# The scan stage with backward tokens in 32-row blocks, and block turns of 128 partitions

## The reference, cut to what matters

```python
m = jnp.einsum('bnihk,bnjhk->bnhij', k_beta, k) * jnp.exp(jnp.where(strict, diff, -jnp.inf))
t_inv = lax.linalg.triangular_solve(m, eye, left_side=True, lower=True, unit_diagonal=True)
u = jnp.einsum('bnhij,bnjhv->bnihv', t_inv, v * beta[..., None])
w = jnp.einsum('bnhij,bnjhk->bnihk', t_inv, k_beta * jnp.exp(g)[..., None])
```

## Time and profile before

| what | value |
| --- | --- |
| runs, median (lowest to highest) | 4532.65 us (4531.85 to 4542.73) |
| profiled execution, span | 4535.4 us |
| PE busy over the span | 3940.0 us (87%) |
| DVE busy | 2176.8 us (48%) |
| ACT busy | 970.4 us (21%) |
| POOL busy | 1048.6 us (23%) |
| scan stages | 571 to 1140 us and 2802 to 3370 us |

### The profile page before, as it was taken

The page is one execution under the profiler, slowest core; times in us unless marked ns, Lnnn a source line. Parts: engine busy times, 40 slices in busy tenths (PEclk is TensorE's granted clock), DMA queues, the critical chain, the costliest instruction groups (busy, mean ns, idle before and its releaser), DMA issues. The chain is left out here.

```text
span 4535.4 us, 81543 instructions
## 1 busy us (share of the span) xinstructions
PE 3940.0 (87%) x34010; PEld 3088.9 (68%) x34010; DVE 2176.8 (48%) x4932; ACT 970.4 (21%) x1898; POOL 1048.6 (23%) x1092
## 2 busy tenths in 40 slices
PE   4999967888777999999779997788869599999994
PEld 3444546676347999999744444566654399999994
DVE  3335046566555445444453341566646544454444
ACT  2233134444110000000033322443431100000001
POOL 0036034453210000011040440445512001000003
PEclk9999978888888999999989998888879799999997
DMA  7556353331528999999664653243233299999995
GB/s 266 173 192 229 127 125 77 77 71 36 192 72 243 276 276 270 280 278 269 183 233 150 241 192 89 71 95 78 66 110 129 105 278 270 274 278 276 271 279 179
DMA packets 822587, 836.27 MB, mean 184 GB/s; under 512 B 92008, under 2 KB 667560, under 8 KB 816076
## 3 DMA queue, kind: packets, MB, share of 16 engines
q1 hardware_dynamic: 740172, 711.10, 52.5%
q10 hardware_dynamic: 70432, 81.03, 5.3%
q0 software_dynamic: 11616, 38.94, 3.8%
HBM read 698.83 MB, written 132.10 MB: 183 GB/s over the span
## 5 line engine op out<-in xcount | busy, mean ns | idle before, releaser
L2525 PE MATMUL ffn_hb<-ffn_xT,ffn_w 128*128 128x144 f32 x8192 | 1055.4, 288 | 11.2 <-DVE ffn_xT L2638 6.5
L2525 PEld LDWEIGHTS ffn_hb<-ffn_xT,ffn_w 128*128 128x128 f32 x8192 | 1025.8, 191 | 14.1 <-DVE ffn_xT L2638 6.7
L521 PE MATMUL front_acc<-front_w,front_xmT 128*128 128x512 f32 (+2 forms) x2304 | 879.2, 541 | 17.7 <-DVE front_xmT L782 17.5
L521 PEld LDWEIGHTS front_acc<-front_w,front_xmT 128*128 128x128 f32 x2304 | 438.2, 192 | 444.7 <-issue 417.7
L2533 PE MATMUL ffn_acc<-ffn_hT,ffn_w 128*128 128x144 f32 x4096 | 550.2, 288 | 0.0
L2533 PEld LDWEIGHTS ffn_acc<-ffn_hT,ffn_w 128*128 128x128 f32 x4096 | 521.4, 191 | 0.8
L2573 ACT ACTIVATE ffn_en<-ffn_hb 128x144 f32<-128x144 f32 x256 | 74.6, 291 | 1483.0 <-PE ffn_hb L2525 1483.0
L2457 POOL DMA_INDIRECT ffn_xe<-scratch_xhat,ffn_g_idx x34 | 34.5, 1015 | 1376.2 <-DVEq L2627 1376.2
L2672 DVE TENSOR_TENSOR ffn_hT<-ffn_en,ffn_hb 128x144 f32<-128x144 f32 x256 | 77.7, 304 | 528.8 <-ACT ffn_en L2573 527.9
L2247 PE MATMUL mixer_acc<-mixer_wout,mixer_oT 128*128 128x512 f32 x576 | 256.6, 604 | 3.2 <-DMA mixer_wout<-in_w_out 1.7
L2596 DVE TENSOR_SCALAR_CACHE_REDUCE ffn_junk<-ffn_row,ffn_pair 128x128 f32<-128x128 f32 (+2 forms) x324 | 245.4, 757 | 6.3 <-DVE ffn_yp L2645 4.9
(11 more groups left out here) (324 smaller groups left out, 5206.0 us busy)
## 6 DMA issues: line engine op xcount, KB each, us to landing
ffn_w<-in_w_e SPq DMA_DIRECT2D x768, 512.0 KB, 6.4
x_res<-in_w_mod SPq DMA_DIRECT2D x40, 1024.0 KB, 5.6
x_res<-scratch_proj SPq DMA_DIRECT2D x36, 768.0 KB, 6.2
scratch_proj<-front_out ACTq DMA_DIRECT2D x90, 256.0 KB, 2.2
ffn_row<-scratch_affT SPq DMA_DIRECT2D x36, 576.0 KB, 6.3
front_w<-in_w_in ACTq DMA_DIRECT2D x8, 2048.0 KB, 12.3
scan_qk<-scratch_qkv SPq DMA_DIRECT2D x16, 1024.0 KB, 9.8
scratch_qkv<-x_res SPq DMA_DIRECT2D x18, 768.0 KB, 3.5
```

The costliest lines, as they stand in the source:

```text
L521: mm = pe.matmul(acc[:, U % 2, 0:size], xmT[:, k, t * P:(t + 1) * P], w[:, n % 2, k, 0:size], start=k == 0, stop=k == KD - 1)
L2525: mm = pe.matmul(hb[:, b, i * CAP:(i + 1) * CAP], w[:, r, k, :], xT[:, s, k, :], start=k == 0, stop=k == KD - 1)
```

## The change

Backward tokens are no longer in reverse over the whole chunk: within each block of 32 rows the order is the scan's, and the two blocks of a chunk stay in storage order. The backward source becomes two blocks of 32 reversed rows, one DMA for each chunk, so a load of n chunks is one forward and n backward DMAs (`pieces`), 79 issues more per layer. The masks on the host follow the new order. Forward and backward now have their 32x32 blocks in such places that `block_in` is two transposes of 128 partitions, into NB and Tb, and a predicated copy of Tb's odd blocks into NB; `inverse_for_x` is one transpose in place of two, `inverse` two in place of four, which fill all of TT; POOL then sets two blocks of TT to zero (`zero_l`, for which `weights` waits). In groups 1 to 4 `block_scaled` follows `block_in` ahead of the attention unit that stood between, both `gla_state` steps stand ahead of `inverse_for_x`, and `turn_keys` of the first half stands ahead of `small`. In group 0 the four `first_latents` between the blocks follow `block_in`. The memset of TT at the start falls away; `odd` is filled by three small ones.

```diff
         betaT, odd = st.sb("betaT", [P, 32]), st.sb("odd", [P, 1])
...
+        pieces = lambda n: [(0, 0, n)] + [(1, m, 1) for m in range(n)]
+        landed = lambda groups: 16 * sum(len(pieces(chunks[g])) for g in groups) + 1
...
-                    src = T[name][r:r + n, c0:c1].rearrange("(m t) c -> t m c", t=CH)
-                    return src[:, ::-1, :] if d else src
+                    x = T[name][r:r + n, c0:c1]
+                    if d:
+                        return x.rearrange("(q t) c -> q t c", q=2)[:, ::-1, :]
+                    return x.rearrange("(m t) c -> t m c", t=CH)
...
-                        sp.wait_ge(tb_v, 2 * (g - 1) + 1)
-                    n = chunks[g] * CH
-                    for d in range(2):
-                        dst = lambda x: x[half(d), g % 2, 0:chunks[g] * H].rearrange("p (m h) -> p m h", h=H)
-                        sp.dma_start(dst(beta), rows("gates", d, first[g] * CH, n, d * H, (d + 1) * H)).then_inc(gate_in[g % 2], 16)
...
+                        sp.wait_ge(tt_v, 2 * (g - 1) + 1)
+                    for d, m, n in pieces(chunks[g]):
+                        at, c = (first[g] + m) * CH, slice(m * H, (m + n) * H)
+                        dst = lambda x: x[half(d), g % 2, c].rearrange("p (m h) -> p m h", h=H)
+                        sp.dma_start(dst(beta), rows("gates", d, at, n * CH, d * H, (d + 1) * H)).then_inc(gate_in[g % 2], 16)
...
-                    for d in range(2):
-                        sp.dma_start(qk[half(d), 0:chunks[g]], rows("qkv", d, first[g] * CH, chunks[g] * CH, 0, 2 * DQ)).then_inc(qk_in, 16)
+                    for d, m, n in pieces(chunks[g]):
+                        sp.dma_start(qk[half(d), m:m + n], rows("qkv", d, (first[g] + m) * CH, n * CH, 0, 2 * DQ)).then_inc(qk_in, 16)
...
-                    for d in range(2):
-                        sp.dma_start(gin[half(d)], rows("proj", d, h * P, P, C_GQ, C_GLR)).then_inc(gl_in, 16)
-                        sp.dma_start(E[half(d)], rows("gla_la", d, h * P, P, d * GQ, (d + 1) * GQ)).then_inc(gl_in, 16)
+                    for d, m, n in pieces(2):
+                        at = h * P + m * CH
+                        sp.dma_start(gin[half(d), m:m + n], rows("proj", d, at, n * CH, C_GQ, C_GLR)).then_inc(gl_in, 16)
+                        sp.dma_start(E[half(d), m:m + n], rows("gla_la", d, at, n * CH, d * GQ, (d + 1) * GQ)).then_inc(gl_in, 16)
...
-                        sp.dma_start(dst[:, 0, :], od[half(d), c % 2].rearrange("p h e -> p (h e)")).then_inc(od_out[c % 2], 16)
+                        sp.dma_start(dst, od[half(d), c % 2].rearrange("p h e -> p (h e)").unsqueeze(1)).then_inc(od_out[c % 2], 16)
...
-                        pe.wait_ge(ta_v, 2 * g + 3)
+                        pe.wait_ge(tt_v, 2 * g + 3)
...
-                        pe.wait_ge(tb_v, 2 * g + 3)
+                        pe.wait_ge(zero_l, 2 * g + 3)
...
-                        for i in range(n):
-                            turn_keys(g, i)
+                        turn_keys(g, 0)
+                        small(g)
+                        turn_keys(g, 1)
...
                     pool.sem_inc(sub_done, 1)
+                    pool.wait_ge(tt_v, 2 * g + 3)
+                    for d in range(2):
+                        pool.memset(TT[after[d], :, late_cols[1 - d]], 0.0).then_inc(zero_l, 1)
+                        pool.wait_ge(zero_l, 2 * g + d + 2)
                     if g + 1 < GROUPS:
                         spread_gates(g + 1)
...
-                def block_in(g, quads):
...
-                    for q in quads:
-                        c = 32 * (q % 2)
-                        out = NB[quad(q)] if q < 2 else NB[quad(q)].rearrange("p r j -> p j r")
-                        dve.transpose(out, PM[quad(q), :, c:c + 32].rearrange("p b i -> p i b")).then_inc(own, step())
+                def block_in(g):
...
+                    for out, c in ((NB, 0), (Tb, 32)):
+                        dve.transpose(out[:], PM[:, :, c:c + 32].rearrange("p b i -> p i b")).then_inc(own, step())
+                    dve.transpose(betaT[:], beta[:, g % 2, :]).then_inc(own, step())
+                    dve.wait_ge(own, step.n)
+                    dve.copy_predicated(NB[:], odd[:].unsqueeze(2).to_broadcast([P, 32, 32]).bitcast(U32), Tb[:]).then_inc(own, step())
...
-                    for q in (0, 3):
-                        rows, cols = solved(q)
-                        dve.transpose(NB[quad(q)].rearrange("p b c -> p c b"), cols).then_inc(nb_v, 1)
...
+                    dve.transpose(NB[:].rearrange("p b c -> p c b"), Tb[:]).then_inc(nb_v, 1)
+
+                def inverse():
+                    for cols in late_cols:
+                        dve.transpose(TT[:, :, cols].rearrange("p b i -> p i b"), Tb[:].rearrange("p c i -> p i c")).then_inc(tt_v, 1)
...
-                        for j in range(4):
-                            block_in(g, (j,))
-                            first_latents(6 + j)
+                        block_in(g)
+                        first_latents(6)
                         block_scaled()
+                        for j in range(7, 10):
+                            first_latents(j)
...
-                        block_in(g, (0, 1))
+                        block_in(g)
+                        block_scaled()
                         attend(at + (g == 1))
-                        block_in(g, (2, 3))
-                        block_scaled()
...
                     if g:
+                        gla_state(h, 0)
+                        gla_state(h, 1)
                         inverse_for_x(g)
-                        gla_state(h, 0)
-                        inverse(1, ta_v)
...
-                        inverse(0, tb_v)
-                        inverse(3, tb_v)
+                        inverse()
```

More of the change, by code:

```diff
@@ L1077, in load_v @@
                         sp.wait_ge(av_p, first[g - 1] + 1)
-                    for d in range(2):
-                        dst = v[half(d), g % 2, 0:chunks[g]].rearrange("p m h e -> p m (h e)")
-                        sp.dma_start(dst, rows("qkv", d, first[g] * CH, chunks[g] * CH, 2 * DQ, 3 * DQ)).then_inc(v_in[g % 2], 16)
+                    for d, m, n in pieces(chunks[g]):
+                        dst = v[half(d), g % 2, m:m + n].rearrange("p m h e -> p m (h e)")
+                        sp.dma_start(dst, rows("qkv", d, (first[g] + m) * CH, n * CH, 2 * DQ, 3 * DQ)).then_inc(v_in[g % 2], 16)
                 def load_gla(h):
@@ L1161, in small @@
                     n = chunks[g] * H
-                    pe.wait_ge(gate_in[g % 2], 64 * (g // 2) + 65)
+                    pe.wait_ge(gate_in[g % 2], 2 * landed(range(g % 2, g + 1, 2)) - 1)
                     pe.wait_ge(RD_v, 2 * g + 3)
@@ L1175, in turn_keys @@
                     if i == 0:
-                        pe.wait_ge(qk_in, 32 * g + 33)
+                        pe.wait_ge(qk_in, landed(range(g + 1)))
                         if g:
@@ L1252, in values @@
                         pe.wait_ge(Z_a, 2 * halves[g][-1] + 3)
-                        pe.wait_ge(v_in[g % 2], 32 * (g // 2) + 33)
+                        pe.wait_ge(v_in[g % 2], landed(range(g % 2, g + 1, 2)))
                     else:
@@ L1715, in _ @@
                     else:
-                        for i in range(n):
-                            turned(g, i, 0, kT_p, kT_a)
+                        turned(g, 0, 0, kT_p, kT_a)
+                        small(g)
+                        turned(g, 1, 0, kT_p, kT_a)
                         for i in range(n):
@@ L1775, in spread_gates @@
                     n = chunks[g] * H
-                    pool.wait_ge(gate_in[g % 2], 64 * (g // 2) + 65)
+                    pool.wait_ge(gate_in[g % 2], 2 * landed(range(g % 2, g + 1, 2)) - 1)
                     if g:
@@ L1783, in scaled_keys @@
                         pool.wait_ge(eg_a, g + 2)
-                        pool.wait_ge(qk_in, 32 * g + 33)
+                        pool.wait_ge(qk_in, landed(range(g + 1)))
                         if g:
@@ L1828, in state_gates @@
                 def state_gates(g):
-                    dve.wait_ge(gate_in[g % 2], 64 * (g // 2) + 65)
+                    dve.wait_ge(gate_in[g % 2], 2 * landed(range(g % 2, g + 1, 2)) - 1)
                     for d in range(2):
@@ L1979, in settle @@
                     step.restart()
-                for x in (TT[:], RD[:], gA[:], beta[:, 0, 16:], PM[:, 16:]):
+                for x in (RD[:], gA[:], beta[:, 0, 16:], PM[:, 16:]):
                     dve.memset(x, 0.0).then_inc(own, step())
+                dve.memset(odd[:], 0.0).then_inc(own, step())
+                dve.wait_ge(own, step.n)
+                for part in (1, 3):
+                    dve.memset(odd[quad(part)], 1.0).then_inc(own, step())
                 dve.memset(S[:, 0], 0.0).then_inc(own, step())
@@ L2783, in host_constants @@
     same = j // CH == i // CH
```

(5 more changed lines are left out.)

53 lines of the change are left out of this document (18 added, 35 removed).

## The result

The changed kernel takes 4674.69 us (median of 4 runs, 4670.40 to 4687.97), the kernel before 4532.25 us in the same comparison. The ratio is 1.0321, with a 95% interval of 1.0306 to 1.0335: slower by 142 us. The forecast was 4645, in a range of 4490 to 4715.

A forecast was written before the change was run, and what follows sets the result against it. PE's fixed order waiting on late results bounds the scan stage; late backward loads on two engines, less the gains, sum to +56 us a layer, +112, giving 4645 us against the median. Range 4490 to 4715.

The forecast's parts named there:

- a first dimension of 2 leaves two engines with all of a backward transfer: Backward loads: transfers divide along the source's first dimension, now 2; by it 4645 us, by the other reading 4498.
- The reading of the affT store: Trace's store of 18 rows: nine engines took two rows each, read as division along the first dimension.
- 18.4, 20.7, 21.0 and 8.6 us late: Second GLA half's load in groups 1 to 4 lands that long after PE needs it, queued on two engines.
- +6.5 + 3.5 - 4.5 = +5.5: Group 0, us a layer: qk load 6.5 late, first_latents behind the block turns lose 3.5, group's end gains 4.5.
- a line through two rows: DMA cost per row and engine, from 8-KB and 2-KB stages: 0.049 us + 0.034 us/KB, 0.18 us for 4 KB.
- the 51.5 forecast: Group 1: GLA half lands 0.3 + 12.8 + 23.5 + 14.9 = 51.5 us after qk's issue, at 775.6.
- the signs named: Profile signs of being right: L1378 waits some 20 us, qk landings 25 us and over, DMA share near 2/16, five transposes.
- The first rival: All sixteen engines carry the backward loads, so the gains stand: 17.3 us a layer, 4498 us; chance 0.25.
- With the state moved ahead: Ends of groups 2 to 4: state steps before the solve's transposes start weights 7.8, 3.2 and 5.6 us sooner.
- the 2.3 us of the solve's earlier start: Attention unit moved behind block_scaled: its 2.3 us on DVE are part of sub_in coming 5.1 us sooner.
- The price of the turn of keys: Group starts: turn_keys(0) ahead of small saves 0.55 us at each of four starts, 2.2 a layer.
- Transposes, copy, memsets: DVE and POOL: 128x1024 transpose 2.05 us, copy_predicated 1.3 us, POOL's 32x1024 memset 1.5 us.

The follow-up runs named there:

- The first experiment: Changed kernel with the backward source cut into 16 pieces instead of 2, so all sixteen engines carry it: 4489.22 us, ratio 0.9896.
- the time with four: Changed kernel with the backward source's first dimension 4 instead of 2: 4541.63 us, ratio 1.0023.
- POOL's queue: Changed kernel, state steps back between the transposes, backward pieces of qk, gin and E issued by POOL instead of SP, first dimension still 2: 4578.61 us.
- qk alone: Changed kernel with first dimension 16 for all backward loads but qk, which keeps 2: 4610.34 us, ratio 1.0171.
- the gates alone at 2: Changed kernel with first dimension 16 for all backward loads but the gates, which keep 2: 4487.94 us, ratio 0.9894.
- 4473 against 4471: Attention unit of groups 1 to 4 put back ahead of block_scaled, against the sixteen-engine kernel with the old state order: 4473.12 against 4471.01 us.
- the 4471-us kernel: Changed kernel with first dimension 16 and, in groups 1 to 4, the state steps put back between the transposes: 4471.01 us, ratio 0.9856.

## Why the prediction was right

**The cause.** The step that carried the sum, "a first dimension of 2 leaves two engines with all of a backward transfer", holds. The first experiment turns it alone: 185 us come and go with it. The share of 0.13 and the packet counts show the two engines, 0.26 the four, and the time with four lies between. POOL's queue, with the same rows and the same 2, speaks against the rows' order in memory as the cause: there the loads aren't bound to two engines. The reading of the affT store as division along the first dimension was right, and so is the sentence of the Trainium skill, "DMA: Bandwidth & Descriptors", section "Why a DMA increments its semaphore by 16 and not by 1", which was weighed beside it. The same section says that a transfer of the software path with fewer than 16 engines takes them from a cursor that goes round, while the hardware path takes the lowest-numbered. Here POOL's queue is the software one and SP's a hardware one, and the shares of 33.0% for POOL's and 0.13 for SP's agree; which engines SP's two are no run here shows.

**The size.** Forecast +112, measured +142. Groups 1 to 4 were forecast at 51 us a layer and measured 42.6 and 47.9. The four waits for E behind them, forecast as 18.4, 20.7, 21.0 and 8.6 us late, are 23.0, 15.7, 15.9 and 8.8 in the first layer. What was mis-sized is group 0, "+6.5 + 3.5 - 4.5 = +5.5", which measured 20.1 and 25.5. Two things are in it. qk was 10.6 us late (L1188 at 594.39, L1182 at 583.80), not 6.5. And the 15.2 us at L1357 (2.0 before), which the sum doesn't have. The profile names no releaser for it, but ACT's queue shows what is late:

```profile
650.54 0.37 ACTq L1639 DMA_DIRECT2D scratch_qT<-x_res  x1
...
661.58 1.30 ACTq L1643 DMA_DIRECT2D x_res<-scratch_qT  x3
```

ACT stores the attention queries and reads them back. From the last store's issue to the read it takes 11.0 us, and 6.0 more to the scores at 667.59; with sixteen engines 2.7 (639.07 to 641.80) and 2.0. That these transfers stand behind the backward pieces on shared engines I conclude from qk alone bringing the wait back (8.6 us) and sixteen engines taking it away.

**The rates.** I took a line through two rows, some 22 GB/s an engine for 4-KB rows; the queue moved 26 (52 over two). The line was read wrong. The windows of the earlier trace rows are not of 8-KB and 2-KB rows: of the first's 753 packets over 512 B only 274 have 8 KB or more, the mean is 5.6 KB, and in the third 12825 of 14012 are under 2 KB, the mean 0.8 KB. Through these means the same two rates give some 25 GB/s for 4 KB, and for a 32-byte row 0.02 us instead of 0.05, an estimate too; it fits that the gates alone at 2 cost nothing. Against it, SP's issues stand still for up to 12.3 us when much is queued, which I had at 0.62 each. The landing in group 1, 47.1 us after qk's issue (746.19 to 793.32), came out close to the 51.5 forecast with both errors in it, and that is luck. Of the signs named, the landing of the qk pieces can't be read: the profile gives none for these loads.

**The gains.** The first rival, sixteen engines at 4498, was measured at 4489: 44 us gained against 35. The sum is near, its attribution is not. "With the state moved ahead" `weights` was to start 7.8, 3.2 and 5.6 us sooner in groups 2 to 4. With sixteen engines group 2 did gain 9.7 in the first layer, groups 3 and 4 5.1 and 2.5; but with the state put back the kernel gains 18 us more. The step that failed is that the state's move makes this gain. The rest of the change makes it, and the move takes some back. What in the rest was not taken apart: the 2.3 us of the solve's earlier start that come from the attention unit's place gave nothing (4473 against 4471), and the turn of keys 3.3, so the cheaper transposes are the likely part, beside the new order of group 0. I had computed the chain from PE's readiness for the state, with the transposes behind it, and not the other order with the same transposes. With the old transposes the move is worth some 3 us in all, within the noise, where the same sum gave 8 a layer. The price of the turn of keys, 4.4 us, measured 3.3, not clear of the noise either.

**Transposes, copy, memsets.** As priced: 2.05 us forecast, 1.94 and 2.15 measured; 1.3 and 1.30; and 1.5 against 0.94 for a memset.

The description ahead of the result is wrong in one point, which changes no sum: before, the backward rows of a chunk stood in storage order, and `[:, ::-1, :]` on `t m c` turned the order of the chunks; so the first dimension was 64 rows, but not reversed ones. The change is what turns the rows within 32.

## What to carry to other kernels

When an access pattern is reshaped, read the size of its first dimension before anything else: at 2 a load had 52 GB/s, at 16 it was hidden. A transfer that is slow on few engines also delays other transfers (PE waited 43.0 us for E on sixteen engines when qk had two, 3.0 when qk had sixteen too) and the issues behind it (12.28 us for one). And when a wait is moved out of the way, compute both orders with the new durations: a reordering that was worth some 3 us with dear transposes cost 18 with cheap ones.

## What the runs showed of the hardware that was not expected

An issue on SP took up to 12.28 us in the first stage when the two engines it feeds were behind, and at most 1.76 for the same loads on sixteen. The number of engines shows in the count of packets under 512 B: one more a transfer for each engine more (576 for 288 transfers from 2 to 4). PE was granted 0.50 in the 11 us of idleness ahead of 793 us and 0.58 over the ten after; one wait of 1.74 us ahead of X went with 0.50 for the 7.7 us behind it, where X and Z without it had 0.85, and X's 128 matmuls took 3.62 us against 2.21. POOL's transfers with a first dimension of 2 had 33.0% of the engines' time, SP's 0.13. PE's busy time for the same matmuls was 3928.5 us in the 4471-us kernel, 3934.8 in the 4489-us one and 3957.1 in the changed kernel. Small rows of 32 bytes on two engines, 512 a group, cost nothing that the time shows when all else is spread (4487.94 against 4489.22).
